# Key scores of each pair of heads as a strand of their own in the written order of a planned kernel

## The reference

```python
def peer(xn, wq, k1, k2, u_tab, v_tab):
    q = (xt @ wq).reshape(t, PEER_HEADS, D_KEY)          # 8 heads, 256 columns each
    q1, q2 = q[..., :D_HALF], q[..., D_HALF:]
    s1 = jnp.einsum("thd,hnd->thn", q1, k1).astype(jnp.float32)   # key scores
    s2 = jnp.einsum("thd,hnd->thn", q2, k2).astype(jnp.float32)
    v1, i1 = lax.top_k(s1, TOPK)
    v2, i2 = lax.top_k(s2, TOPK)
    cand = (v1[..., :, None] + v2[..., None, :]).reshape(t, PEER_HEADS, TOPK * TOPK)
    sv, ci = lax.top_k(cand, TOPK)
    ...
    hid = jax.nn.gelu(jnp.einsum("td,tkd->tk", xi, u_tab[ei]))
    return jnp.einsum("tk,tkd->td", gi * hid, v_tab[ei])
```

## Time and profile before

| | us |
|---|---|
| three runs | 2060.1, 2061.18, 2061.55 |
| median | 2061.18 |
| span of the profiled execution, first to last instruction | 2060.5 |
| TensorE (PE) busy | 1673.1 (81%) |
| VectorE (DVE) busy | 1409.5 (68%) |
| ScalarE (ACT) busy | 807.0 (39%) |
| GpSimd (POOL) busy | 616.3 (30%) |
| moved by DMA | 774.28 MB, mean 376 GB/s |

### The profile page before, as it was taken

One profiled execution on the slowest core, in us unless ns is written; L12 is line 12 of the kernel. 1 busy time (PEld: TensorE's weight loads), 2 busy tenths in 40 slices (PEclk: granted clock), 3 DMA queues, 4 the chain that ended last, 5 costly groups with the idle time before them and its releaser, 6 DMA issues.

```text
span 2060.5 us, 20758 instructions
## 1 busy us (share of the span) xinstructions
PE 1673.1 (81%) x6664; PEld 967.5 (47%) x6664; DVE 1409.5 (68%) x3610; ACT 807.0 (39%) x2063; POOL 616.3 (30%) x516
## 2 busy tenths in 40 slices
PE   8989989999889988887779678777887876665555
PEld 4449856583477464463337234533643542221111
DVE  4324337468775478668887777788887698877776
ACT  2423213434478236423443553234455234332222
POOL 0000000021422214522443463244333434454551
PEclk9999999999999999898989989898998998877777
DMA  9676867479999999999999999999999999999996
GB/s 387 212 270 240 293 232 272 163 265 411 388 419 419 420 419 417 389 420 418 420 419 406 420 420 419 413 406 420 418 400 405 410 390 420 420 420 420 420 420 288
DMA packets 108958, 774.28 MB, mean 376 GB/s; under 512 B 12208, under 2 KB 12720, under 8 KB 16432
## 3 DMA queue, kind: packets, MB, share of 16 engines
q0 software_dynamic: 73728, 536.90, 63.3%
q1 hardware_dynamic: 35120, 236.04, 29.5%
HBM read 771.85 MB, written 1.05 MB: 375 GB/s over the span
## 4 chain that ended last, share of the span: by engine, by line
PE 41%; DMA 35%; DVE 9%; issue 6%; ACT 6%; POOL 3%; SPq 0%; DVEq 0%; POOLq 0%
PE psum L1104 12%; DMA ring<-in_slabs_dram 10%; DMA arena<-in_peer_dram,eidx 10%; DMA ring<-in_peer_dram,eidx 9%; PE psum L745 8%; PE psum L764 8%; PE psum L949 6%; DMA kv<-in_peer_dram,eidx 5%; PE psum L966 3%; DVE x L2018 1%; DVE arena L2008 1%; POOL arena L2160 1%; ACT diag L1436 1%; POOL ring L2160 1%; ACT L1426 1%
## 5 line engine op out<-in xcount | busy, mean ns | idle before, releaser
L2160 POOL DMA_INDIRECT arena<-in_peer_dram,eidx x202 | 241.9, 1198 | 857.0 <-DVE eidx L1880 440.7
L1104 PE MATMUL psum<-arena,diag 128*128 128x512 f32 x580 | 325.0, 695 | 110.5 <-ACT diag L1436 110.2
L1426 ACT ACTIVATE wexp<-hid 128x1 f32<-128x1 f32 x512 | 102.9, 201 | 653.8 <-DVE hid L2008 652.6
L2008 DVE CUSTOM_DVE_ANT_0 arena<-arena,osb 128x1024 f32<-128x1024 f32 x202 | 245.0, 1221 | 60.3 <-DMA arena<-in_peer_dram,eidx 59.5
L745 PE MATMUL psum<-ring,hT 128*128 128x512 f32 x560 | 261.3, 617 | 17.4 <-DMA ring<-in_slabs_dram 14.6
L1104 PEld LDWEIGHTS psum<-arena,diag 128*128 128x128 f32 x580 | 119.1, 217 | 289.2 <-ACT diag L1436 166.9
L1104 PE MATMUL psum<-ring,diag 128*128 128x512 f32 x384 | 206.0, 667 | 59.6 <-ACT diag L1436 59.4
L2160 POOL DMA_INDIRECT ring<-in_peer_dram,eidx x152 | 178.7, 1175 | 235.1 <-PE psum L1104 167.9
L2008 DVE CUSTOM_DVE_ANT_0 ring<-ring,osb 128x1024 f32<-128x1024 f32 x152 | 184.9, 1221 | 61.8 <-DMA ring<-in_peer_dram,eidx 61.1
L764 PE MATMUL psum<-hT,ring 128*128 128x128 f32 x1536 | 186.8, 283 | 24.2 <-DMA ring<-in_slabs_dram 22.3
L764 PEld LDWEIGHTS psum<-hT,ring 128*128 128x128 f32 x1536 | 183.3, 199 | 37.6 <-DMA ring<-in_slabs_dram 26.6
(11 more groups left out here) (324 smaller groups left out, 2100.5 us busy)
## 6 DMA issues: line engine op xcount, KB each, us to landing
ring<-in_slabs_dram SPq DMA_DIRECT2D x208, 1024.0 KB, 9.5
ring<-in_slabs_dram SPq DMA_DIRECT2D x8, 768.0 KB, 4.5
arena<-in_peer_dram,eidx POOLq DMA_INDIRECT x202, 17.2
ring<-in_peer_dram,eidx POOLq DMA_INDIRECT x152, 17.2
ring<-in_slabs_dram SPq DMA_DIRECT2D x4, 512.0 KB, 4.4
kk<-in_keys_dram SPq DMA_DIRECT2D x2, 1024.0 KB, 8.7
kv<-in_peer_dram,eidx POOLq DMA_INDIRECT x104, 16.3
rowg<-in_rows_dram SPq DMA_DIRECT2D x3, 512.0 KB, 13.8
```

Of the source, the lines that this page charges most:

```text
L1104: ins = pe.matmul(bank(b), diags_of(n), pair(slot_of[n])[:, 1024 + 512 * h:1536 + 512 * h], start=(k == 0), stop=(k == 127))
L1426: act.activation(wn, hid[:, 128 * t + k:128 * t + k + 1], ACT.Gelu_apprx_tanh).then_inc(*up("gelu", n))
L2008: v.tensor_tensor_reduce(out=row, in0=row, in1=row_y[t], scale=1.0, scalar=0.0, op0=ALU.mult, op1=ALU.add, accum_out=hid[:, c:c + 1]).then ...
L2160: pool.indirect_dma_start(pair(i), None, tables, bass.IndirectOffsetOnAxis(ap=eidx[:, 128 * t + k:128 * t + k + 1], axis=0)).then_inc(sig. ...
```

## The change

`key_scores` becomes a strand of its own, K00, K01, K10 and K11, in the list of stages right behind its mixer's M; the four head pairs follow one another in it. Its wish is 1.0, below that of every other strand. Stage M on TensorE now holds the four query tiles alone. On ScalarE and VectorE the strand is empty. All strands behind it in `STAGES` move by one to four places. Waits, signals and PSUM banks of each key-score step are those of before.

```diff
--- before.py
+++ after.py
@@ -547,7 +547,7 @@
                     return 0.9 if len(gathers) > 128 * tile + 32 * routed - T_AHEAD else 1.5
                 if e == "PE" and s == "M00" and at_step["PE", "B1"] < (T_HEAD if at_step["PE", "M00"] < T_QUERY else T_ATT):
                     return 1.3
-                return 1 + 0.01 * i
+                return 1.0 if s[0] == "K" else 1 + 0.01 * i
@@ -705,8 +705,8 @@
-        STAGES = ("B0", "G0", "M00", "R00", "C00", "B1", "Q00", "M01", "R01", "C01", "Q01", "M10", "R10", "C10", "Q10",
-                  "M11", "R11", "C11", "Q11", "F0", "F1")
+        STAGES = ("B0", "G0", "M00", "K00", "R00", "C00", "B1", "Q00", "M01", "K01", "R01", "C01", "Q01", "M10", "K10", "R10", "C10",
+                  "Q10", "M11", "K11", "R11", "C11", "Q11", "F0", "F1")
@@ -1050,15 +1050,18 @@
-                for c in range(5):
-                    if c < 4:
-                        b = b_[(1, 3)[c % 2]]
-                        yield from feature_tile(s, b, hTt, "wq", s, c)
-                        bank_free[b] = at("qp", s, c)
-                    if c:
-                        yield from key_scores(s, c - 1)
-
-            def key_scores(s, hh):
+                for c in range(4):
+                    b = b_[(1, 3)[c % 2]]
+                    yield from feature_tile(s, b, hTt, "wq", s, c)
+                    bank_free[b] = at("qp", s, c)
+
+            def key_scores(l, t):
+
+                s = "M%d%d" % (l, t)
+                for hh in range(4):
+                    yield from two_heads(s, hh)
+
+            def two_heads(s, hh):
@@ -1117,6 +1120,7 @@
+            stage.update({"K%d%d" % o: key_scores(*o) for o in ORDER})
@@ -1449,6 +1453,7 @@
+            stage.update({"K%d%d" % o: iter(()) for o in ORDER})
```

## The result

The changed kernel has a median of 2067.48 us (2065.07 to 2072.19, 6 runs) against 2060.44 (2055.89 to 2061.55, 6 runs) for the kernel before; the ratio on record is 1.0043 with a 95% interval of 1.0033 to 1.0053 (the two medians alone give 1.0034). So it is 6 to 9 us slower, where I had forecast 5.4 us faster; the time lies within the range and on the side of the slower rival. The profiled execution took 2066.6 us, of which 2064.8 are the span.

A forecast was written before the change was run, and what follows sets the result against it. TensorE was taken to bound the kernel up to 441 us, the DMA engines from 450; 2061.2 - 2.5 (first gather) - 2.9 (later mixers' holes) = 2055.8 us. Its own range was 2051 to 2059, the whole range 2047 to 2068.

The forecast's parts named there:

- slower rival: Block 1's attention, 414 to 445 us: route 0 holds up attention, TensorE idles 5.6 to 8 us; 2066.8 us, chance 0.25.
- Parts 1 to 3: Tile (0,0): no added work, scores of pair 0 10.4 us earlier, first gather at about 430 us; gain 2.5 us.
- Part 4: Block 1's attention on VectorE: 22 us of query tiles on TensorE cover 15.8 us of route 0; cost nought.
- Part 5: Tiles (0,1), (1,0), (1,1): route 0 moves into VectorE's idle time, later DMA holes shrink; gain 2.9 us.
- first hole: DMA engines at 377 and 360 GB/s from 1330 to 1350 us, 2.4 us lost; expected to get smaller.
- The second: DMA hole from 1680 to 1700 us, 3.4 us lost, laid to route 1 on VectorE; expected to get smaller.
- Part 6: Everything after 413 us: the greedy planner may reorder all engines; booked as nought, with +-4 us kept in the range.
- rival "no change": Whole kernel: ScalarE's order keeps routes 1 to 3 in place, DMA holes merely move; 2057.2 to 2065 us, chance 0.25.

The follow-up runs named there:

- e4: Changed kernel with T_SOON 0 instead of 10, so early dots, weights and downs go behind every stage; 2067.75 us, ratio 1.0026.
- e10: Changed kernel with dots, weights and downs behind everything until block 1's attention is over, urgent again afterwards; 2065.86 us, ratio 1.0019.
- e8: Changed kernel with route 0 alone put behind block 1's attention on VectorE; 2059.87 us, ratio 1.0006.
- e6: Changed kernel with block 1's steps, first query copy to attention's end, ahead of everything on VectorE and ScalarE; 2060.94 us, ratio 1.0009.
- e2: Changed kernel with the key-score strand kept only for tiles (0,1), (1,0), (1,1), tile (0,0) as before; 2059.95 us, ratio 1.0000.
- e5: Kernel before with T_SOON 0 instead of 10, so early dots, weights and downs lose their urgency; 2063.36 us, ratio 1.0018.
- e7: Kernel before with the same edit as e6, block 1's attention ahead of everything on VectorE and ScalarE; 2063.04 us, ratio 1.0019.
- e12: Kernel before, key scores still between query tiles, with the two edits of e11; 2063.82 us, ratio 1.0026.
- e11: e8 with ScalarE's exponential of pair 0 moved from the mixer's strand to the routes' strand; 2055.88 us, ratio 0.9976.

## Why the prediction was wrong

**Parts 1 to 3, the scores and the first gather: right.** Key scores of pair 0 at 414.30 (I had said 412.8), of pair 1 at 424.44 (424), first gather at 434.20 (430), since route 0 began at 417.21 and not at 414. The gate exponential is still right behind query copy 3: 441.04, 441.53. The mean of 430 to 450 us rose to 308 GB/s, above the 250 I had asked for. The price I put on it, one gather or 2.5 us, looks even low for that moment (1.6 MB, 3.9 us by 440), but nearly half of it is slabs that came before 430; all of it was given back twice over in the next 100 us.

**Part 4, the cover: the step that failed.** I set the 15.8 us of route 0 against 22 us of query tiles and booked nought. TensorE did use the tiles as cover and had no hole until 445. When route 0 was done at 433.19 only 5.8 us of query tiles were left (the records at 433.37 and 437.16), and attention, whose scores of 416.56 were read by VectorE only at 429.26, had several rounds between the engines to go. The error was to take route 0 for the whole block and the tiles for its cover alone. Once route 0 has run, the first gather leaves and lands, and with it come a dot, weights with their table loads, the gates and the first piece of route 1, all taken ahead of attention. By then (441) the query tiles are used up, and attention's last unit is not even scored. The cover was counted against the first thing that moved, and not against what that thing holds up and sets off. Both signs of being wrong that I had named for this place came: TensorE idle before 450 (from 445.28) and attention ending after 445 (at 465.36).

The slower rival had the place and the picture (query tiles used up, attention one behind the other) but put 5.6 to 8 us on it; TensorE idled 11.29 + 4.39 = 15.7 us there, block 1 fell back by 11.6, and the kernel by 6 to 9. It also wanted less than 16 us of query tiles left when the route starts: some 20 us were left, and the hole came all the same. I gave it 0.25, and its 2066.8 stands near the measured time partly by luck: by bytes, half of the loss is made by the gathers' pause after 500 us, which no part of the prediction has, and e4 and e10 lose as many bytes with a hole of 3 us (342 and 344 GB/s from 440 to 540 us, against 345). e8 and e6 settle where the loss comes from: with route 0 behind attention it is gone. They don't settle the path.

**Part 5, the later mixers: the mechanism half right, its worth wrong.** VectorE's waits for the first key scores are gone in two of the three mixers (0.35 us instead of 4.42 in mixer (1,1), none in (1,0)) and down to 3.71 us from 6.08 in (0,1). The first hole closed: from 1320 to 1350 us the changed kernel moves 420 GB/s, where the kernel before had 385, worth 2.5 us. The second grew instead of shrinking by half. GpSimd and windows of the changed kernel, beside the earlier trace rows:

```profile
1649.60 0.50 DVE L1808 MAX8 sm<-psum 128x8 f32<-128x128 f32 x2 [0.35 <-PE psum L1073]
...
1672.54 1.83 POOL L2166 DMA_INDIRECT kv<-in_peer_dram,eidx  x1 [12.23 <-PE psum L1107]
...
1700.69 1.43 POOL L2166 DMA_INDIRECT early<-in_peer_dram,eidx  x1 [12.09 <-PE psum L1107]
...
1690.00:1700.00 10.00, 3.37 (x4) 1.51 (x5) 9.62 (x32) 3.18 (x11) 0.00 (x0) 0.53 0.41 172
```

The gathers stop twice as before, 12.23 us in route 0 and 12.09 in route 1 (13.65 and 9.66 before), and the second stop brings the DMA engines to 172 GB/s; from 1660 to 1720 us the holes cost 10.5 us of transfer, against 3.6 before. e2 shows the same pair (420 GB/s in the first, 315 from 1680 to 1700 against 348), and puts this term at 0.0000 with 0.0013 either way, where I had -0.0014. Route 1 was the part that mattered, and I had said myself that it doesn't move; taking half of 5.9 us had no row behind it. I had also written that the slabs had the DMA engines alone from 1650 to 1660. That reading doesn't hold: the last gather before that pause left at 1647.21, and gathers took 17 us from issue to landing on the median of the profile's page. The Trainium skill ("DMA: Bandwidth & Descriptors", section "Queues, rings and completion order") has each DMA engine go round between the queues that have work. No run here shows what that rule would make of the time, since the traces give no share of each queue in a full stretch.

**Part 6, the plan's luck: sized about right.** From 540 to 2040 us the two kernels moved data equally fast, 415 GB/s, although holes appeared and went at half a dozen places. e5, e7 and e12, edits that should have cost little or nothing, were 3 to 5 us slower. One size of the sum was off without effect: I put 0.7 us around the span, by comparing times with the span of another execution; in each run of the changed kernel it is 1.8 us.

**The rival "no change"** describes the kernel once route 0 is kept behind attention (e6, e8), and e2. Its reason, ScalarE's order, is what e11 removed.

**What stays open.** The 40 us pause of the gathers in e4 and e10: the downs were behind block 1's slabs on TensorE, but I ran nothing that frees them alone. For the same reason it is open how much of the changed kernel's own loss comes of the 21 us pause before 535.28 and how much of TensorE's hole. And the share of e11's gain that is luck of the plan: e11 and e12 differ in their whole order after 413 us, not only in the stops shown.

## What to carry to other kernels

Before a step is moved forward, follow what its result releases, not only its own time: here a result that came 7 us sooner set off work of high priority on two other engines, in front of the chain that was the bound at that moment. Count a cover against all that is set off, not against the first piece. And where a saturated resource follows a stretch bound by something else, judge the edit by the bytes moved up to the seam; here the earlier first request won 1.6 MB up to 440 us and 3.8 MB were lost in the 100 us behind it. And when one edit removes a hole, check that the time follows: e4 and e10 took most of TensorE's hole away and stayed slow. Finally, an operand that was ready earlier was worth nothing here while another engine's fixed order still held the next consumer; the two belonged in one change (e11), and each alone was nought or a loss (e8, e12).

## What the runs showed of the hardware

The TensorE clock fell where the hole was: the windows from 450 to 470 us show a granted clock of 0.50 and 0.57 in the changed kernel, where TensorE waited from 445.28 to 456.57 and again before 465.36; 0.50 is the lower of its two levels, 1.2 GHz. Attention's four transposes at 456.57 took 1.09 us, where four of the same shape took 0.66 at 443.79, so the hole also slows what comes right after it. Loads of ScalarE's tables took 1.28 us each, and mixing attention's exponential with the experts' weights brought three of them into 11 us (442.26, 448.94, 451.27). An identical kernel differed by 12 to 15 us from run to run on three of the chips, which is more than anything this change did.
